# Experts in groups of four, gathered and scattered by stream, and another order in the opening, in a two-stack transformer kernel

## The reference, cut to what matters

```python
def expert_choice_ffn(h, w_router, w_g, w_u, w_d):
    B, n, D = h.shape
    cap = CAPACITY_FACTOR * n // N_EXPERTS          # 32 tokens an expert
    logits = jnp.einsum('bnd,de->ben', h, w_router)
    aff = jax.nn.softmax(logits, axis=1)
    gate, idx = lax.top_k(aff, cap)
    xs = h[bi, idx]                                 # gather
    a = jnp.einsum('becd,edf->becf', xs, w_g)
    u = jnp.einsum('becd,edf->becf', xs, w_u)
    y = jnp.einsum('becf,efd->becd', jax.nn.silu(a) * u, w_d)
    return jnp.zeros_like(h).at[bi, idx].add(y * gate[..., None])   # scatter
...
for l in range(DEPTH):
    mod = silu_c @ w_ada[l] + b_ada[l]              # shift, scale and gate rows of each layer
    ...
    x = x + gt2 * expert_choice_ffn(h2, w_router[l], w_e_gate[l], w_e_up[l], w_e_down[l])
    if not last:
        ...
        xc = xc + gtc2 * expert_choice_ffn(hc2, w_router[l], w_e_gate[l], w_e_up[l], w_e_down[l])
```

## Time and profile before

| | us |
|---|---|
| median of 3 runs | 3191.61 (3187.85 to 3193.98) |
| the profiled execution | 3193.48 |
| its span, first to last instruction | 3191.7 |

### The profile page before, as it was taken

How to read it: one execution, slowest core, us unless ns; L and a number is a source line. 1 busy time by engine, 2 the same in 40 slices (tenths; PEclk the granted TensorE clock), 3 DMA queues, 4 the chain that set the end, 5 groups by cost and what they waited for, 6 DMA issues and landing times.

```text
span 3191.7 us, 30572 instructions
## 1 busy us (share of the span) xinstructions
PE 2865.7 (90%) x11844; PEld 1771.8 (56%) x11844; DVE 1090.2 (34%) x2436; ACT 654.2 (20%) x1242; POOL 3.9 (0%) x10
## 2 busy tenths in 40 slices
PE   3999998999999989899997999889879898898898
PEld 2677887768888434344445333343356587333333
DVE  6421651531660355754342111121235632111111
ACT  2421211321220452330002000100253301111011
POOL 0000000000000000000000000000000000000000
PEclk9999999999999989889997999999998898899999
DMA  7613564605554011304151799998612364799998
GB/s 314 280 63 158 211 242 155 263 30 231 202 220 184 31 49 53 132 18 194 53 211 53 319 390 395 386 393 357 285 53 80 137 259 158 318 428 429 428 429 348
DMA packets 51927, 712.96 MB, mean 223 GB/s; under 512 B 5554, under 2 KB 7874, under 8 KB 8820
## 3 DMA queue, kind: packets, MB, share of 16 engines
q1 hardware_dynamic: 51028, 708.49, 54.2%
q0 software_dynamic: 800, 3.11, 0.2%
HBM read 710.53 MB, written 1.05 MB: 223 GB/s over the span
## 4 chain that ended last, share of the span: by engine, by line
PE 82%; DVE 6%; ACT 5%; issue 4%; DMA 2%; SPq 0%; PEldq 0%; ACTq 0%; DVEq 0%
PE bank L553 81%; DMA ring<-weights 2%; PE bank L552 2%; ACT work L1203 1%; ACT work L1200 1%; ACT L1007 1%; DVE work L1287 1%; DVE work L1288 1%; ACT work L1007 0%; ACT work L1008 0%; DVE work L1282 0%; DVE small L1464 0%; DVE work L1481 0%; DVE work L1344 0%; ACT work L1202 0%
## 5 line engine op out<-in xcount | busy, mean ns | idle before, releaser
L553 PE MATMUL bank<-h,ring 128*128 128x256 f32 (+1 forms) x3840 | 1030.6, 429 | 45.2 <-ACT h L1014 37.2
L553 PEld LDWEIGHTS bank<-h,ring 128*128 128x128 f32 x3840 | 741.3, 194 | 317.9 <-issue 197.1
L553 PE MATMUL bank<-ring,work 128*64 128x512 f32 x3072 | 699.0, 614 | 77.8 <-PEq L766 44.4
L553 PEld LDWEIGHTS bank<-ring,work 128*64 128x64 f32 x3072 | 224.3, 142 | 520.2 <-issue 483.9
L553 PE MATMUL bank<-work,ring 128*128 128x256 f32 (+1 forms) x1728 | 452.1, 419 | 3.2 <-issue 3.2
L553 PE MATMUL bank<-work 128*128 128x64 f32 (+5 forms) x1760 | 378.1, 409 | 32.6 <-ACT work L1203 16.0
L553 PEld LDWEIGHTS bank<-work,ring 128*128 128x128 f32 x1728 | 327.8, 190 | 116.9 <-issue 80.8
L553 PEld LDWEIGHTS bank<-work 128*128 128x128 f32 (+2 forms) x1760 | 241.2, 201 | 148.2 <-issue 108.0
L1306 DVE SCALAR_TENSOR_TENSOR X<-bank,mod,X 128x256 f32<-128x256 f32 x248 | 109.5, 481 | 545.8 <-PE bank L553 545.8
L1262 DVE SCALAR_TENSOR_TENSOR ring<-ring,crow 128x1024 f32<-128x1024 f32 x192 | 228.4, 1221 | 13.0 <-DMA ring<-weights 12.7
L1601 DVE TENSOR_TENSOR work<-bank,work 128x512 f32<-128x512 f32 x32 | 22.1, 692 | 467.7 <-ACT work L1197 467.7
(11 more groups left out here) (166 smaller groups left out, 1424.3 us busy)
## 6 DMA issues: line engine op xcount, KB each, us to landing
ring<-weights SPq DMA_DIRECT2D x336, 2048.0 KB, 13.5
crow<-c_rows POOLq DMA_DIRECT2D x2, 512.0 KB, 13.2
X<-x_cols SPq DMA_DIRECT2D x1, 1024.0 KB, 16.5
X<-x_cols POOLq DMA_DIRECT2D x1, 1024.0 KB, 17.5
out<-X SPq DMA_DIRECT2D x1, 1024.0 KB, 4.5
cst<-const SPq DMA_DIRECT2D x1, 897.5 KB, 6.9
cst<-const POOLq DMA_DIRECT2D x1, 768.0 KB, 24.1
crow<-c_rows SPq DMA_DIRECT2D x1, 512.0 KB, 4.3
```

The costliest lines, as they stand in the source:

```text
L553: nc.tensor.matmul(o, l, r, start=start, stop=stop)
```

## The change

In the expert loops a pass now takes four experts (`GROUP` = 4, `GROUPS` = 4 a layer). The slots of `xs` lie by expert, stream and slot (8 x 256 columns); the answers `ye` lie by stream, so a scatter product has 128 rows (4 experts x 32 slots) and the 256 columns of one stream, 16 products a pass for two streams and 8 for one. The transposes and down of an expert stand behind half of, and behind, the next expert's gate and up, and the gathers of the next group stand around the last expert's. The one-hot matrix `pk` is made once a layer for all 16 experts: DVE spreads the slot numbers (`eachrow`), PE spreads them over the partitions ("bc"), DVE compares with the token's number. So `pick` and its copy go, and the gather reads `pk` at a column that depends on the pass, an address in a register. The order of the chunks follows the experts. In the opening the three condition rows come as one row of 12 KB to one partition (`craw`), PE spreads them in six products of 512 columns with `ones` (job "row"), ACT and DVE make silu from them, the angles follow, and then the sixteen modulation products. The tokens' load stands behind chunk 1, and POOL's load of `pars2` waits for "lat".

```diff
-TRIPS = {"a0": 1, "b1": 2, "d0": 1, "e0": PAIRS, "d1": 1, "e1": PAIRS}
+TRIPS = {"a0": 1, "b1": 2, "d0": 1, "e0": GROUPS, "d1": 1, "e1": GROUPS}
...
-        out = [x for e in range(2) for x in (("eg", e), ("eu", e))] + [x for e in range(2) for x in (("eh", e), ("ey", e))]
-        out += [("pick", 0)] + each("scat", KT) + each("xs", 2)
+        out = [("eg", 0), ("eu", 0)]
+        for e in range(1, GROUP):
+            out += [("eg", e), ("eu", e), ("eh", e - 1), ("ey", e - 1)]
+        out += [("eh", GROUP - 1), ("ey", GROUP - 1)] + each("xs", KT) + each("scat", KT)
...
-            sp_.dma_start(crow[:, 0, :], c_rows[0:1, :].partition_broadcast(P)).then_inc(c_in, 16)
+            sp_.dma_start(craw, c_rows).then_inc(c_in, 16)
...
+            R.phase("b1", 0)
+            pool.wait_ge(*R.evac("lat", 3))
             pool.dma_start(pars2[:, :, :], par2).then_inc(second_in, 16)
...
-            def gather(nt):
-
-                pe.wait_ge(*R.evac("pick"))
-                for g in range(2):
-                    groups = []
-                    for d in range(4):
-                        for s in range(nt // T):
-                            cols = slots_of(R.bank("xs", g)[:, d * P:(d + 1) * P], s)
-                            groups.append((cols, [(htok[:, 2 * s + i, (4 * g + d) * P:(4 * g + d + 1) * P],
-                                                   slots_of(pk[:, 2 * s + i], s)) for i in range(2)]))
-                    product("xs", g, groups)
+            def gather(d, nt, first):
+
+                slots = R.bank("xs", d)[:, 0:2 * P].rearrange("p (e r) -> p e r", r=64)
+                product("xs", d, [(slots[:, :, 32 * s:32 * s + 32], [
+                    (htok[:, 2 * s + i, d * P:(d + 1) * P], pk[:, 2 * s + i, bass.ds(first, P)].rearrange("p (e r) -> p e r", r=32))
+                    for i in range(2)]) for s in range(nt // T)])
...
+                gate_up(0, range(4))
+                for e in range(1, GROUP):
+                    gate_up(e, range(2))
+                    hidden(e - 1)
+                    gate_up(e, range(2, 4))
+                    down(e - 1)
+                gather(0, nt, g * P + P)
+                hidden(GROUP - 1)
+                gather(1, nt, g * P + P)
+                gather(2, nt, g * P + P)
+                down(GROUP - 1)
+                for d in range(3, KT):
+                    gather(d, nt, g * P + P)
+                pe.wait_ge(*R.evac("ey", GROUP - 1))
+                pe.wait_ge(*picked_ready.take())
+                for t in range(KT):
+                    product("scat", t, [(R.bank("scat", t)[:, s * T:(s + 1) * T], [(ye[:, s, t * P:(t + 1) * P], og[:, s])])
+                                        for s in range(nt // T)])
...
+            for j in range(6):
+                product("row", j, [(R.bank("row", j)[:, :], [(ones[0:1, :], craw[:, 512 * j:512 * j + 512])])])
...
-                (TS(seli[0:32, 0:32], eidx[0:32, :], 1.0, const_of("ctxrow")[0:32], ALU.mult, ALU.add)
-                 .then_inc(*slots_ready.inc()))
+                settle_to(nc.vector.tensor_copy(seli[0:32, 0:32], eidx[0:32, :]), slots_ready)
+                TT(eachrow[0:32], seli[0:32, 0:32].unsqueeze(1).to_broadcast([32, 32, CAP]),
+                   const_of("mine")[0:32].unsqueeze(2).to_broadcast([32, 32, CAP]), ALU.mult).then_inc(*rows_ready.inc())
...
+                nc.vector.memset(pk[:, :, GROUPS * P:], 0.0)
+                if layer:
+                    nc.vector.memset(xs[:, :, :], 0.0)
...
+                for s in range(nt // T):
+                    dve.wait_ge(*R.full("bc", s))
+                    for i in range(2):
+                        ins = TS(pk[:, 2 * s + i, 0:GROUPS * P], R.bank("bc", s)[:, :], const_of("tokid", i, 1), None, ALU.is_equal)
+                    ins.then_inc(*R.freed("bc", s))
...
+            for j in range(6):
+                act.wait_ge(*R.full("row", j))
+                A(csig[:, j], R.bank("row", j)[:, :], ACT.Sigmoid).then_inc(*c_ready.inc())
...
-            modulate(shares("a0", ""), spent)
+            for j in range(6):
+                dve.wait_ge(*c_ready.take())
+                TT(crow[:, j // 2, 512 * (j % 2):512 * (j % 2) + 512], R.bank("row", j)[:, :], csig[:, j], ALU.mult)\
+                    .then_inc(*R.freed("row", j))
...
             settle(TS(trig[:, 1], trig[:, 1], const_of("sign"), None, ALU.mult))
+            modulate(shares("a0", ""), spent)
```

More of the change, by code:

```diff
@@ L41 @@
 CAP = 32
[L42 removed]
+GROUP = 4
+GROUPS = E // GROUP
 BIG = -1e30
[L45 removed]
+TRIPS = {"a0": 1, "b1": 2, "d0": 1, "e0": GROUPS, "d1": 1, "e1": GROUPS}
 PHASES = ["a0", "b1", "d0", "e0", "d1", "e1"]
@@ L140, in plan @@
     if phase == "a0":
-        return []
+        return each("row", 6) + each("pad", 2)
     if phase == "b1":
@@ L184, in plan_chunks @@
         return out + each("out", 2) + [("router", 0)]
-    return [("gu", i) for i in range(8)] + each("dn", 4)
+    out = each("gu", 4)
+    for e in range(1, GROUP):
+        out += [("gu", 4 * e + i) for i in range(4)] + [("dn", 2 * (e - 1) + i) for i in range(2)]
+    return out + [("dn", 2 * (GROUP - 1) + i) for i in range(2)]
 CHUNK_PLANS = {ph: plan_chunks(ph) for ph in PHASES}
@@ L855, in dense @@
                 turned("cols", 0, [(R.bank("cols")[0:64, 0:32], seli[0:32, :])])
-                pick(nt)
-                gather(nt)
-                pe.wait_ge(*R.evac("xs", 1))
+                pe.wait_ge(*rows_ready.take())
+                for s in range(nt // T):
+                    product("bc", s, [(R.bank("bc", s)[:, :], [(ones[0:32, :], eachrow[0:32, 16 * s:16 * s + 16].rearrange("p e r -> p (e r)"))])])
+                pe.wait_ge(*R.evac("htok", 2 * nt // P - 1))
+                pe.wait_ge(*R.evac("bc", nt // T - 1))
+                for d in range(KT):
+                    gather(d, nt, 0)
+                pe.wait_ge(*R.evac("xs", KT - 1))
                 flush()
@@ L945, in experts, with hidden, down @@
                         used.append(c)
-                for e in range(2):
+                def hidden(e):
                     pe.wait_ge(*R.evac("eu", e))
-                    turned("eh", e, [(R.bank("eh", e)[:, j * P:(j + 1) * P], ae[:, e, j * P:(j + 1) * P]) for j in range(4)])
+                    turned("eh", e, [(R.bank("eh", e)[:, j * P:(j + 1) * P], ae[:, e % 2, j * P:(j + 1) * P]) for j in range(4)])
+                def down(e):
                     pe.wait_ge(*R.evac("eh", e))
@@ L981, in _ @@
                 dense(layer)
-                with pe.Fori(0, PAIRS) as p:
-                    book.enter(f"e{layer}", p)
-                    R.phase(f"e{layer}", p)
-                    experts(layer)
-                    book.leave(f"e{layer}", PAIRS)
+                with pe.Fori(0, GROUPS) as g:
+                    book.enter(f"e{layer}", g)
+                    R.phase(f"e{layer}", g)
+                    experts(layer, g)
+                    book.leave(f"e{layer}", GROUPS)
         @block.scalar
@@ L1574, in merge, with gathered @@
                     dve.wait_ge(*R.evac("bra", KT - 1))
[L1576 to L1585 removed]
+            def gathered(nt):
+                for d in range(KT):
+                    dve.wait_ge(*R.full("xs", d))
@@ L1593, in experts @@
+                    ins.then_inc(*R.freed("xs", d))
+            def experts(layer, g):
                 nt = 2 * T if layer == 0 else T
-                iota = const_of("iota")[:, 0:nt]
-                onehot(nt, idxc[:, bass.ds(p + 1, 1)])
-                TS(og[:, 0:nt], iota, idxc[:, bass.ds(p, 1)], gatec[:, bass.ds(p, 1)], ALU.is_equal, ALU.mult)\
-                    .then_inc(*picked_ready.inc())
-                for e in range(2):
+                for s in range(nt // T):
+                    ins = TS(og[:, s], const_of("iota"), idxc[:, s, bass.ds(g, 1)], gatec[:, s, bass.ds(g, 1)], ALU.is_equal, ALU.mult)
+                ins.then_inc(*picked_ready.inc())
+                for e in range(GROUP):
@@ L1616, in _ @@
+            dve.wait_ge(*R.evac("row", 5))
             dve.wait_ge(const_in, 16)
@@ L1643, in _ @@
                 dense(layer)
-                with dve.Fori(0, PAIRS) as p:
-                    book.enter(f"e{layer}", p)
-                    R.phase(f"e{layer}", p)
-                    experts(layer, p)
-                    book.leave(f"e{layer}", PAIRS)
+                with dve.Fori(0, GROUPS) as g:
+                    book.enter(f"e{layer}", g)
+                    R.phase(f"e{layer}", g)
+                    experts(layer, g)
+                    book.leave(f"e{layer}", GROUPS)
         book.start("end")
```

164 lines of the change are left out of this document (74 added, 90 removed).

## The result

The changed kernel takes 3117.17 us, the median of four runs (3114.95 to 3117.56); before took 3190.95 beside it. The ratio is 0.9767, with a 95% interval from 0.975 to 0.9784: faster by 73.8 us. The forecast was 3131 with a range from 3116 to 3151, so the sign held, and the mechanism in layer 0 too, and 14 us more were gained than worked out. The profiled execution took 3117.14 us.

A forecast was written before the change was run, and what follows sets the result against it. PE was taken to bound layer 0's expert loop, the weights layer 1's, DVE's chain the opening. From 3193.48 us, -11.1 - 52.4 + 3.0 - 0.8 = -61.3 gave 3132.2, as a median about 3131, range 3116 to 3151.

The forecast's parts named there:

- The weights become the bound of layer 0: Layer 0's expert loop: PE 110.4 us a group against 117.6 of DMA; layer 1's sum of squares starts 52.4 us earlier.
- the register term: Gathers in the expert loop: a register address costs 0.1 us per pair, +3.2 us a group, bounds 0 and 0.76 per pair.
- PE's group, 110.4 us: Layer 0's expert loop: PE's summed time for a group of four experts, against 117.6 us of DMA.
- Layer 1 is bound by the weights: Layer 1's expert loop before the change: the DMA runs at 428 GB/s for 400 us without a gap.
- e1: Layer 1's expert loop: no gain but at the end, -0.8 us, between -3 and +3.
- The turn 2.8: End of each pass of the expert loop: a 2.8 us wait that comes four times, not eight.
- Ahead of the loops: Work before each expert loop: added DVE steps cost +2.3 us in layer 0 and +3.0 in layer 1.
- the gather itself keeps its time: at half clock: Gather ahead of each loop: 0.211 us an instruction, for 128 columns as for 64 before, so no change.
- Opening: Start of the kernel: DVE takes the sum of squares at 45.9 us, -11.1 us, bounds -16 and -6.
- (a): Layer 0's expert loop: PE stays the bound through costlier register addresses, total 3159 to 3192 us; chance 6%.
- (b): Layer 0's expert loop: DMA misses layer 1's 428 GB/s; slower than before from 376 GB/s, 3200 us at 370; chance 1.5%.
- (c): Both expert loops: PE's waits for chunks lower its clock, about 3870 us at half clock throughout; 2% for a slower kernel.

The follow-up runs named there:

- halved chunks: Chunks issued in the loop load only half their columns: the kernel before so edited took 3180.26 us, the changed kernel so edited 2956.65 us.
- the constant-address run: The changed kernel with the loops' gather reading `pk` at a constant column instead of a register address: 3112.68 us.
- its repetition: The changed kernel run once more, without any edit, on the chip of a later run: 3118.6 us.
- the kernel without interleaving: The changed kernel with each expert's gate and up whole, then its transposes and down, and all eight gathers behind the last down: 3124.4 us.
- the spread gathers: The changed kernel with angles before four silu rows, and three gathers a group among the last expert's gate and up and the third's down: 3109.92 us.
- the experts alone: The changed kernel with the opening of the kernel before, so only the expert part of the change: 3130.98 us.
- the angles ahead: The changed kernel with the opening's angles put after the first two silu rows, ahead of the other four: 3113.32 us.
- the scatter moved: The changed kernel with halved chunks and the eight scatter products ahead of the last five gathers: 104.0 us for the first group, then 105.6 and 105.5.

## Why the prediction was right, and where its sizes were off

**The weights become the bound of layer 0: right.** Windows, chain and the runs with halved chunks all show it. e0 from its first product to its last took 465.1 us, forecast 467.3 (1762.9 to 2230.2); 2.0 of these 2.2 us are the register term in the five gathers of the tail, since 72 instructions took 11.64 us where the sum had 13.6.

**PE's group, 110.4 us: mis-sized, 99.8 measured.** It changed the result little only because the DMA hid it. Products on chunks: 384 instructions in 83.2 us, where I had 86.9, -3.7. Most of it is that the 29.2 us of the earlier trace rows contain the products behind the turn, at a lower clock (128 such instructions at 1.00 take 27.7), and this goes with the idle turn; the rest is the end of each row, which overlaps with the next. The three microseconds behind a turn of before, in a window:

```profile
1827.25:1830.25 3.00, 3.00 (x8) 0.94 (x10) 0.00 (x0) 0.00 (x0) 0.00 (x0) 0.57 0.45 191
```

The other terms: register addresses 3.2: none, by the constant-address run. The turn 2.8: none. ACT ahead of the scatter 0.4: none. Transposes 2.2 for 2.6. Gather and scatter 14.45 for 14.5: the 0.12 us an instruction of 128 columns was right. The sum of these is -10.6.

**"Layer 1 is bound by the weights": wrong for the kernel before.** A DMA without a gap was taken for the bound, but with halved chunks a pass still took 58.0 us. PE and the weights (58.8) were so close there that both were busy throughout. The forecast of e1 didn't suffer, since it rests on when the last chunk lands, and in the changed kernel PE needs 92.8 us of 117.6.

**Ahead of the loops: the extra DVE work was right, the gather was not.** It came 2.2 and 3.2 us later (forecast 2.3 and 3.0). But "the gather itself keeps its time: at half clock" failed. Timeline of the change ahead of e1, and windows over the gather ahead of e0:

```profile
2644.84 5.23 PE L561 MATMUL bank<-work 128*128 128x128 f32 x32 [3.33 <-issue]
2650.84 1.51 PE L561 MATMUL bank<-ring,work 128*64 128x512 f32 x6 [0.77 <-DVE work L1621]
...
1731.30:1736.30 5.00, 4.98 (x23) 5.00 (x24) 0.85 (x2) 0.00 (x0) 0.00 (x0) 0.50 0.00 0
1736.30:1741.30 5.00, 4.84 (x43) 4.65 (x41) 2.24 (x6) 0.00 (x0) 0.00 (x0) 0.98 0.00 0
```

The clock was 0.50 in the first of these windows and 0.98 in the next, where before it stayed at 0.50 to 0.55 for all 13.5 us of the earlier trace rows. I had applied the old clock to new instructions. That is -3.7 and -1.9 us. The second is not firm: the gather ahead of e1 took 5.23 to 5.25 us in the change, its repetition, the kernel without interleaving, the spread gathers and the halved chunks, and 6.68 to 6.72 with the experts alone, the constant address, the angles ahead and the scatter moved, and in these four the stretch of d1 that the table follows took 396.4 to 396.7, in the other five 398.2 to 400.6. The entry of e1, 0.77 instead of 2.81, gives 2.0 more.

**Opening: right in its steps, -12.3 for -11.1.** The steps of the change, by their rows:

```profile
6.15 10.61 PE L561 MATMUL bank<-work,cst 1*128 1x512 f32 x12 [6.15 <-DMA cst<-const]
17.42 0.69 DVE L1644 TENSOR_TENSOR crow<-bank,work 128x512 f32<-128x512 f32 x1 [1.01 <-ACT work L1242]
18.14 0.29 DVE L1650 CAST work<-work 128x256 f32<-128x256 int32 x1
25.61 1.23 DVE L1295 SCALAR_TENSOR_TENSOR ring<-ring,crow 128x1024 f32<-128x1024 f32 x1
27.61 6.47 PE L561 MATMUL bank<-h,cst 128*128 128x256 f32 x16 [10.85 <-ACT h L1026]
49.90 29.75 PE L561 MATMUL bank<-h,ring 128*128 128x256 f32 x128 [15.82 <-ACT h L1039]
```

Silu of all rows was done at 18.1 (forecast 18.7), the angles at 25.6 (26.1), the products at 44.0 (44.5), PE's sum of squares long before (forecast "done by 36", measured 34.1). Only the constants landed sooner, at 6.1 instead of 6.9.

**e1: right, -1.3 for -0.8.** **The rivals.** (a) fell with the register's address at zero; (b) and (c) fell in the windows: 428 GB/s and 1.00. Only one core runs here. On (b), the Trainium skill's figure of 358 GB/s a core ("DMA: Bandwidth & Descriptors", "Where 436 GB/s comes from") is not what this core does in either loop. On (c), PE waited 0.5 to 1.6 us, mostly 1.24, ahead of 48 of the 96 chunks of e0 and 67 of those of e1, and the granted clock stayed at 1.00. The Trainium skill's rule ("TensorE: Matmul & The Clock Gate", "Loop structure matters more than you think") is of a long DMA wait ahead of every matmul. PE's waits for a DMA in these loops end at 1.6 us, so no run here tests it; it doesn't reach waits of this size. Behind the 2.68 to 3.06 us of the turns of before, which are not waits for a DMA, the granted clock was 0.50 to 0.61 in the next three microseconds, at all 14 turns.

**Slips in its arithmetic, without weight.** 3132.2 less 1.9 is 3130.3, not 3131; the gains at the other end of the bounds add up to 75, not 76; d1's own terms give +3.2, not +3.0. The prices of rival (a), 3159 and 3192, leave out the opening and d1; with them it would have been about 3152 and 3183.

The unforeseen 15 us of the profiled pair are, then: first stack 3.9 (taken for variation), gathers 5.6 (of which 1.9 not firm), e0 2.2, the entry of e1 2.0, opening 1.2, e1 0.5, less 0.6 in d1.

## What to carry to other kernels

In a loop that waits for weights, PE's own cost is hidden to the size of its waits; only what stands behind the last chunk still counts, so put work that uses no chunk between the chunks, and cut the tail. A run with halved loads tells in one look who binds a stage and by how much: here 525.00 against 524.98 us. It is needed even where the DMA shows no gap: layer 1 before looked bound by the weights, and with half the bytes a pass took the same 58.0 us. Before costing a row at the time it had, ask what clock it ran at, and whether the change leaves that gap in place.

## What the runs showed of the hardware that I had not expected

- Matmuls whose operand has its address in a register cost no more than those with a constant one: 11.64 us for 72 either way.
- PE's waits of 0.5 to 1.6 us, ahead of 48 of the 96 chunks of e0 and 67 of the 96 of e1, left the granted clock at 1.00 through both loops.
- The same gap of PE, 2.3 us in 5, is followed by a granted 0.61 in one execution and by 1.00 in another, for 2.9 us. Even within one execution, behind the same wait of 2.67 us at the same place of the loop, 72 instructions took 11.61 us once and 13.24 the next time. d1 alone varied from 396.3 to 400.8 us between kernels with the same code there.
- The gather of 64 instructions ahead of e0 ran at 0.50 to 0.55 throughout when they had 64 columns, and with 128 columns at 0.50 in the first 5 us, at 0.98 in the next. That of 32 ahead of e1 took 5.2 or 6.7 us in kernels alike there. Which of the differences ahead of it or in it does this was not tried.
